# RWKV stage of a two-block transformer kernel: chunk states of pair p beside the inverse of p+1 and the preparation of p+2

## The chip, the cores and the metric

One core of one Trainium2 chip. The metric is the device time of one execution in microseconds (us); lower is better.

## What is computed

Two transformer blocks over 512 tokens of width 1024, in fp32. The change touches one branch of the first block, the RWKV-7 time mix over 16 heads of 64 channels. Its inputs come from a projection and are shifted by a token; then a state of 64x64 per head runs over the tokens:

```python
f = f + (f_prev - f) * mu                       # token shift, per channel
a = sigmoid(a0 + fa @ w_a2); g = sigmoid(fg) @ w_g2
kk = k * k_k; kk = kk / max(norm(kk), 1e-12)    # per head
k = k * (1 + (a - 1) * k_a)
def step(state, (r, w, k, v, kk, a)):           # per head, 512 tokens
    sa = state @ (-kk)
    state = state * w + outer(sa, kk * a) + outer(v, k)
    y = state @ r
y = ((y - mean) * rsqrt(var + 64e-5)) * ln_w + ln_b   # per head
y = (y + sum(r * k * r_k) * v) * g
```

The rest (two attentions, gates, output projections, two feed-forward layers) stays as it is.

## The kernel before

Every engine has its own written-out program; they meet at semaphores, and each engine takes its instructions in program order. Weights come in 126 units of 128x2048 through a ring of 3 places: a DMA, then `hi(n)` on ScalarE rounds a unit to fp32r (L975), GpSimd subtracts to get the low part (L479), and TensorE does three products for each (`mm3`, L488 to L490).

The heads are taken in 8 pairs, a pair over the 128 partitions, its 512 tokens in 4 chunks of 128. The work of a pair:
- *Projection.* `side_unit` gives two weight units (r and k, then v and a gate). One piece is three 512-column products; a unit is 16 pieces. Both go to PSUM banks 0 and 1. ScalarE copies them out (`take_rk`, `take_vg`), and VectorE shifts them by a token (`shift`, L1591, L1592).
- *Preparation* (`prep`): small projections for decay, rate and gate, sums over heads by a product with `ones_head`, ScalarE sigmoids, roots and exponentials, VectorE products. The root of the key norm is a square root and a reciprocal of a 128x512 tile (L1616); the norm of the output has the same (L1691).
- *Tokens and grams*: transposes (L818), then products of 256 columns (L832, L833), taken out of PSUM by `copy_predicated` (L1712).
- *Inverse*: a triangular matrix for each chunk and head is inverted in 7 levels. A level is 8 small products (`level_x`, L732), an addition on VectorE (L1651), 16 products (`level_t`, L742, L744) and four copies on ScalarE (L1200, L1201); VectorE makes the mask product for the next level (`level<-gram,consts`, L1654). Two refining products follow (`refine_u`, `refine_c`).
- *Chunks* (`chunks`): for each of the 4 chunks in turn a right-hand side (L778, L779), its copy on ScalarE, the solution (L785), its copy on VectorE, and the state's update (L791, L792, L1676, L1677). The output of the chunk is L782, L795, L796.
- *Norm* of the output, and gate: L805, L810, L1685 to L1701.

`pair_step` of pair p runs: levels 2 to 6 and refining of p beside the preparation of p+1, the chunks of p, then tokens, grams and levels 0 and 1 of p+1 beside the norm of p. Pieces of the projection of p+2 are put in by `fill(2)` and `fill(1)`. Pairs 6 and 7 have no projection left to put in. Behind the last pair `rwkv_hi` and `rwkv_lo` split all 8 pairs at once, beside the products `attb`; then `rwkvb` follows.

Of the kernel before, what the change touches and what calls it, by code (L numbers as in the profile page):

```python
# [9 lines left out]
F32R = mybir.dt.float32r  # L10
I32 = mybir.dt.int32
# [4 lines left out]
P = 128  # L16
# [10 lines left out]
L2_EPS2 = 1e-24  # L27
# [70 lines left out]
CCOLS = [("ident", P), ("eps", 1), ("ln_eps", 1), ("ones_head", P), ("ones", P), ("strict_incl", 2 * P),  # L98
# [7 lines left out]
N_CCOLS = _c  # L106
TOE_LEN = 640


def constants():  # L110
# [12 lines left out]
    put("strict_incl", np.concatenate([(p <= c), (p < c)], 1).astype(np.float32))  # L123
# [41 lines left out]
def build(nc, x, wpack, lora_wa, lora_g, params, rel_bias, post_gains, sink, ctab, btab, icount, out):  # L165
# [7 lines left out]
    with ExitStack() as ctx:  # L173
# [23 lines left out]
        def sem(name):  # L197
# [14 lines left out]
        C = fixed("consts", [P, N_CCOLS])  # L212
        PR = fixed("params_sb", [P, N_PCOLS])
        stat = fixed("stat", [P, 64])
        OAT = fixed("att_out", [P, 2, T])
        SG = place("gate_act", [P, 2, T], at=top[0] - 4 * 2 * T)[0]
        OAl = place("att_lo", [P, 2, T], F32R, at=top[0] - 4 * 2 * T)[0]
# [13 lines left out]
        G0 = place("gate0_tile", [P, 2, T], at=r.at)[0]  # L231
        LRAW = r("lora_raw", [P, 2, T + 1])
# [7 lines left out]
        ORW = place("rwkv_out", [P, PAIRS, T], at=x_at)[0]  # L240
        r = Region(y_at)
        RAW = r("rkv", [P, 2, 3, T + 1])
# [5 lines left out]
        LM = r("mid_decay", [P, 2, 2, NT])  # L248
        assert r.at <= y_at + 4 * NT * D
# [11 lines left out]
        X2 = r("work_x", [P, T])  # L261
        KB = r("kb", [P, 2, T])
# [3 lines left out]
        GM = [r(f"gram{h}", [P, NT, 4, P]) for h in range(2)]  # L266
# [7 lines left out]
        ORh = place("rwkv_hi", [P, KT, T], F32R, at=base + K16)[0]  # L274
        ORl = place("rwkv_lo", [P, KT, T], F32R, at=base + 2 * K16)[0]
# [53 lines left out]
                             "pt_taken", "pv_full", "o_taken"))  # L329
        sink_in, ic_in, x_back, gain_in, out_done = (  # L330
# [9 lines left out]
        side_taken = sem("side_taken")  # L340
        gate_tile = sem("gate_tile_ready")
        gate_stored = sem("gate_stored")
        pad_ready = sem("pad_ready")
        gate_back = [sem("gate0_back"), sem("gate1_back")]
        gate0_tile, gate0_stored = sem("gate0_tile_ready"), sem("gate0_stored")
        ident_r = sem("ident_r_ready")
        pair_open = sem("pair_open")
        rs = {n: sem(n) for n in ("z_full", "sig_ready", "zg_full", "g_ready", "sq_ready", "ss_full", "nrm_ready", "sqrt_ready",
                                  "rk_ready", "bonus_full", "csm_ready", "exps_ready", "rakb_ready",
# [23 lines left out]
        def side(pair, u):  # L373

            return 1 + 2 * pair + u + (UNITS["gate0"] if pair >= 2 else 0)
# [107 lines left out]
        def _(pe):  # L483
# [175 lines left out]
            def side_unit(j):  # L659
# [3 lines left out]
                if j:  # L663
                    pe.wait_ge(side_taken, j)
# [1281 lines left out]
```

## Time and profile before

| | |
|---|---|
| median of 3 runs | 2293.16 us (2291.77 to 2301.49) |
| profiled execution | 2285.9 us, its span 2284.1 us, mean granted clock 0.922 |
| TensorE busy | 2047.9 us, 90% of the span |
| VectorE busy | 929.9 us, 41% |
| ScalarE busy | 759.3 us, 33% |
| GpSimd busy | 579.3 us, 25% |
| RWKV stage | from 301.5 us, first product of the preparation, to 1005.5 us, first product of `attb` |

A matmul's end is modelled, so TensorE's busy share hides short waits. Start-to-start distances of consecutive instructions tell more. An fp32 product shows as two instructions, an fp32r product as one. The granted clock is a share of 2.4 GHz; a low stretch is at half of that.

### The profile page before, as it was taken

The numbers are of one execution on the slowest core, as the hardware profiler recorded it, in microseconds if no ns is written. First come the engines' busy times: TensorE is split into PE (matmuls) and PEld (weight loads), VectorE is DVE, ScalarE is ACT, GpSimd is POOL, SyncE is SP. The second block draws the span as 40 slices with busy tenths as digits, with TensorE's granted clock in tenths as the row PEclk, the third lists the DMA queues.
The fourth block names the chain that finished last, engine by engine and source line by source line (L and its number), as shares of the span: only waits on it lengthen the run. The fifth ranks groups of instructions, "written<-read, shape, count | busy, mean of one in ns | idle before, by whom it ended". The sixth has DMA issues, their size and how long they took to land.

```text
span 2284.1 us, 23519 instructions
## 1 busy us (share of the span) xinstructions
PE 2047.9 (90%) x9988; PEld 1629.4 (71%) x9988; DVE 929.9 (41%) x1400; ACT 759.3 (33%) x1097; POOL 579.3 (25%) x130
## 2 busy tenths in 40 slices
PE   6999969889888988878799989979898888999897
PEld 5877757667666767756688868867666667888786
DVE  2033366865866864632301134440554322111243
ACT  4234533433433422211422222242455223212222
POOL 2422210010110100003244434424121423444342
PEclk9999989999999975569899999989999999999999
DMA  4611210010100120012222222222111212222221
GB/s 158 211 56 60 79 60 22 26 44 19 44 26 19 44 97 1 0 39 100 79 79 97 106 74 92 93 74 97 38 56 42 106 52 87 105 98 92 76 98 67
DMA packets 31067, 160.66 MB, mean 70 GB/s; under 512 B 3023, under 2 KB 5327, under 8 KB 14708
## 3 DMA queue, kind: packets, MB, share of 16 engines
q1 hardware_dynamic: 19244, 135.53, 16.9%
q10 hardware_dynamic: 11720, 23.63, 3.0%
q8 instruction: 79, 1.29, 0.2%
q14 instruction: 24, 0.20, 0.0%
HBM read 152.57 MB, written 10.25 MB: 71 GB/s over the span
## 4 chain that ended last, share of the span: by engine, by line
PE 76%; DVE 13%; ACT 5%; issue 5%; POOL 1%; POOLq 0%; DMA 0%; DVEq 0%; ACTq 0%
PE ps L488 20%; PE ps L489 19%; PE ps L490 19%; PE ps L573 2%; PE ps L551 2%; PE ps L742 2%; PE ps L732 2%; PE ps L744 2%; ACT w_hi L975 2%; DVE work_t L1698 1%; PE ps L778 1%; PE ps L779 1%; PE ps L785 1%; DVE gram L1712 1%; POOL w_lo L479 1%
## 5 line engine op out<-in xcount | busy, mean ns | idle before, releaser
L479 POOL TENSOR_TENSOR w_lo<-w_raw,w_hi 128x2048 fp32r<-128x2048 f32 x126 | 579.1, 4597 | 1673.7 <-ACT w_hi L975 1673.6
L488 PE MATMUL ps<-ht_hi,w_hi 128*128 128x512 f32 x1240 | 518.6, 418 | 21.8 <-DVE ht_lo L1453 14.0
L490 PE MATMUL ps<-ht_hi,w_lo 128*128 128x512 f32 x1240 | 492.7, 397 | 0.0
L489 PE MATMUL ps<-ht_lo,w_hi 128*128 128x512 f32 x1240 | 492.3, 397 | 0.0
L975 ACT ACTIVATE w_hi<-w_raw 128x2048 fp32r<-128x2048 f32 x126 | 241.2, 1915 | 550.4 <-PE ps L490 519.9
L488 PEld LDWEIGHTS ps<-ht_hi,w_hi 128*128 128x128 f32 x1240 | 238.8, 193 | 98.4 <-issue 40.5
L490 PEld LDWEIGHTS ps<-ht_hi,w_lo 128*128 128x128 f32 x1240 | 238.0, 192 | 52.0
L489 PEld LDWEIGHTS ps<-ht_lo,w_hi 128*128 128x128 f32 x1240 | 239.3, 193 | 46.2 <-issue 4.2
L488 PE MATMUL ps<-w_hi,hid_hi 128*128 128x512 f32 x432 | 173.9, 402 | 24.1 <-DVE hid_lo L1796 16.5
L1796 DVE TENSOR_TENSOR hid_lo<-hidden,hid_hi 128x1024 fp32r<-128x1024 f32 x27 | 114.8, 4264 | 151.8 <-ACT hid_hi L1302 151.8
L489 PE MATMUL ps<-w_lo,hid_hi 128*128 128x512 f32 x432 | 172.8, 400 | 0.0
L490 PE MATMUL ps<-w_hi,hid_lo 128*128 128x512 f32 x432 | 172.8, 400 | 0.0
L488 PEld LDWEIGHTS ps<-w_hi,hid_hi 128*128 128x128 f32 x432 | 83.1, 192 | 45.2 <-issue 17.2
L488 PE MATMUL ps<-w_hi,ht_hi 128*128 128x512 f32 (+2 forms) x256 | 89.5, 350 | 25.4 <-DVE ht_lo L1761 17.6
L1200 ACT ACTIVATE tinv_t<-ps 128x512 fp32r<-128x512 f32 x96 | 57.7, 601 | 137.7 <-PE ps L744 135.0
L489 PEld LDWEIGHTS ps<-w_lo,hid_hi 128*128 128x128 f32 x432 | 83.3, 193 | 19.3
L490 PEld LDWEIGHTS ps<-w_hi,hid_lo 128*128 128x128 f32 x432 | 82.8, 192 | 19.5
L489 PE MATMUL ps<-w_lo,ht_hi 128*128 128x512 f32 (+2 forms) x256 | 88.9, 347 | 0.0
L490 PE MATMUL ps<-w_hi,ht_lo 128*128 128x512 f32 (+2 forms) x256 | 88.7, 346 | 0.0
L1791 DVE TENSOR_TENSOR hidden<-ps,gate_act 128x1024 f32<-128x1024 f32 x16 | 19.6, 1224 | 159.8 <-ACT gate_act L1344 159.8
L732 PEld LDWEIGHTS ps<-tinv,level 128*128 128x128 f32 x384 | 60.6, 227 | 32.0 <-issue 22.2
L732 PE MATMUL ps<-tinv,level 128*128 128x128 f32 x384 | 69.1, 326 | 12.9 <-ACT tinv L1201 6.9
(246 smaller groups left out, 2868.4 us busy)
## 6 DMA issues: line engine op xcount, KB each, us to landing
w_raw<-in_wpack SPq DMA_DIRECT2D x126, 1024.0 KB, 4.8
bias_skewed_dram<-bias_rows_dram ACTq DMA_DIRECT2D x1, 3840.0 KB, 24.2
toe<-bias_skewed_dram ACTq DMA_DIRECT2D x1, 3072.0 KB, 13.8
x_res<-in_x SPq DMA_DIRECT2D x4, 512.0 KB, 5.0
gate_dram<-gate_tile ACTq DMA_DIRECT2D x8, 256.0 KB, 4.5
gate_dram<-gate_tile ACTq DMA_DIRECT2D x4, 512.0 KB, 5.1
merged<-gate_dram ACTq DMA_DIRECT2D x1, 2048.0 KB, 11.4
gate<-gate_dram ACTq DMA_DIRECT2D x1, 2048.0 KB, 12.5
```

What stands on the lines that cost most here:

```text
L479: nc.gpsimd.tensor_tensor(Wl[:, slot, :], raw[:, slot, :], f32(Wh[:, slot, :]), ALU.subtract).then_inc(lo_ready, 1)
L488: mm(dst, wh, ah, start=first, stop=False)
L489: mm(dst, wh, al, start=False, stop=False)
L490: return mm(dst, wl, ah, start=False, stop=last)
L551: last = mm(bank(s["bank"], s["n"]), s["q"], s["k"], start=True, stop=True)
L573: last = mm(out_slot(a, i), v, PT[:, j, :], start=j == 0, stop=j == len(it["vals"]) - 1)
L732: last = mm(ps[:, 4 + h, t * P:(t + 1) * P], Mb[h][:, t, :], Tb[h][:, t, :] if lv else identR[:], start=True, stop=True)
L742: mm(ps[:, 6 + h, t * P:(t + 1) * P], Xb[h][:, t, :], TT[h][:, t, :], start=True, stop=True)
L744: last = mm(ps[:, 4 + h, t * P:(t + 1) * P], TT[h][:, t, :], Xb[h][:, t, :], start=True, stop=True)
L975: actf(Wh[:, n % RING, :], raw[:, n % RING, :], ACT.Copy).then_inc(hi_ready, 1)
L1200: actf(TT[h][:].rearrange("p a b -> p (a b)"), bank(6 + h), ACT.Copy)
L1796: v.tensor_tensor(HIl[:, 2 * g:2 * g + 2, :], HID[:, 2 * g:2 * g + 2, :], f32(HIh[:, g % RING, :, :]), ALU.subtract).then_inc(hid_lo, 1)
```

## The change

All loops of the stage become one `step(p)` for p from -2 to 7 on every engine. In a step the chunks of pair a = p, the whole inverse with tokens and grams of pair b = p+1, and the preparation of pair c = p+2 are put into one another by hand.
- The projection goes by halves of a unit (8 pieces, one output tile), all into bank 0 in the later pairs. Each half waits until the half before it was taken out. `early` are the last two halves of c (v and gate), `late` the first two of c+1 (r and k).
- Token shift at evacuation: ScalarE copies a half, scaled by mu, into one tile (`stage`), and VectorE adds the unscaled part from PSUM, shifted by a token (`shift`, one instruction and a column).
- Head sums for roots become products with the data as weights and 2 columns of `ones_head`, so that a root is 128x8; ScalarE widens it (`widen`) and 4 transposes bring it back (`spread`). Both 128x512 reciprocals go.
- The grams that the inverse needs are made on their own at the start of a step (`inverse_grams`); the other products of 128 columns follow later (`grams`). `refine_u` loses its identity product, and the add after `refine_c` takes twice the old value instead.
- The right-hand sides of both heads share bank 3, with a wait `head_done` between.
- `rwkv_hi` and `rwkv_lo` of pairs 0 to 6 are made before the last step. The reload of `x_res` is issued later, and `absdist` is loaded on its own in the second block.

The core of the diff, indentation as in the file, first TensorE's functions, then ScalarE's, then VectorE's:

```diff
+            def side_half(n, b, behind):
+                u = UNIT0["lora"] + n // 2
+                if n % 2 == 0:
+                    pe.wait_ge(lo_ready, u + 1)
+                if behind >= 0:
+                    pe.wait_ge(*half_taken(behind))
+                for k in range(KT):
+                    wh, wl = rows_of(u, KT, k, n % 2 * P, P)
+                    last = mm3(bank(b), wh, wl, HTh[:, k, :], HTl[:, k, :], k == 0, k == KT - 1)
+                    if k == KT - 1:
+                        last.then_inc(side_full, 1)
+                    yield
...
+            def head_sums(dst, src):
+                for t in range(NT):
+                    last = mm(dst[:, 2 * t:2 * t + 2], src[:, tok(t)], root_cols(ones_head), start=True, stop=True)
+                return last
...
+            def spread(dst):
+                for t in range(NT):
+                    last = nc.tensor.transpose(dst[:, tok(t)], NX[:, tok(t)], ident)
+                return last
...
+            def inverse_grams(b):
+                w("kb1_ready", 1, b, 1)
+                for t in range(NT):
+                    for h in range(2):
+                        last = mm(ps[:, 4 + h, tok(t)], KB[heads(h), 1, tok(t)], RA[b % 2][heads(h), t, 1, :],
+                                  start=True, stop=True)
+                inc(last, "agram_full")
...
+            def step(p):
+                a, b, c = p, p + 1, p + 2
+                has_a, has_b, has_c = 0 <= a, 0 <= b < PAIRS, c < PAIRS
+                if p == -2:
+                    early = later_halves(GATE0 + 6, GATE0 + 8)
+                else:
+                    early = later_halves(half(c, 2), half(c, 2) + (2 if 2 <= c < PAIRS else 0))
+                late = later_halves(half(c + 1, 0), half(c + 1, 0) + (2 if 2 <= c + 1 < PAIRS else 0))
+                if has_b:
+                    inverse_grams(b)
+                if has_c:
+                    lora_z(c, 0)
+                if has_a:
+                    chunk_rhs(a, 0)
+                advance(early, 2)
+                if has_a:
+                    chunk_solve(a, 0)
+                if has_b:
+                    level_x(b, 0)
+                advance(early, 2)
+                if has_a:
+                    chunk_out(a, 0)
+                for t in range(1, NT):
+                    if has_b:
+                        level_x(b, t)
+                    if has_a:
+                        chunk_rhs(a, t)
+                    advance(early, 1)
+                    if has_c:
+                        if t == 1:
+                            lora_z(c, 1)
+                        elif t == 2:
+                            key_sums(c)
+                        else:
+                            key_roots(c)
+                    if has_a:
+                        chunk_solve(a, t)
+                    if has_b:
+                        level_t(b, t)
+                    advance(early, 1)
+                    if has_a:
+                        chunk_out(a, t)
+                    advance(early, 2)
+                if has_b:
+                    level_x(b, 4)
+                    to_tokens(b, 0)
+                    to_tokens(b, 1)
+                advance(late, 1)
+                if has_a:
+                    mean(a)
+                if has_b:
+                    level_t(b, 4)
+                advance(late, 3)
+                if has_b:
+                    level_x(b, 5)
+                    to_tokens(b, 2)
+                advance(late, 1)
+                if has_a:
+                    variance(a)
+                if has_b:
+                    level_t(b, 5)
+                    grams(b, 0)
+                advance(late, 3)
+                if has_b:
+                    level_x(b, 6)
+                    grams(b, 1)
+                advance(late, 1)
+                if has_a:
+                    norm_roots(a)
+                if has_b:
+                    level_t(b, 6)
+                    grams(b, 2)
+                advance(late, 2)
+                if has_c:
+                    gate_z(a, c)
+                advance(late, 1)
+                if has_b:
+                    refine_u(b)
+                    grams(b, 3)
+                advance(late, 2)
+                if has_c:
+                    bonus(c)
+                if has_b:
+                    refine_c(b)
+                advance(late, 2)
+                assert next(early, None) is None and next(late, None) is None
...
+            def stage(n, b, buf, mu):
+                act.wait_ge(side_full, n + 1)
+                actf(buf, bank(b), ACT.Copy, scale=pcol("mu", mu)).then_inc(staged, 1)
...
+            def take_gate1(pair, b):
+                n = half(pair, 3)
+                act.wait_ge(side_full, n + 1)
...
+            def widen(root):
+                return actf(NX[:].rearrange("p (t h c) -> p t h c", h=2, c=HD),
+                            root[:].unsqueeze(3).to_broadcast([P, NT, 2, HD]), ACT.Copy)
...
+            def shift_part(pair, part):
+                if part == 0:
+                    act.wait_ge(gate_stored, 16 * pair)
+                else:
+                    act.wait_ge(*half_taken(half(pair, part) - 1))
+                stage(half(pair, part), 0, GT[:], 8 * part + pair)
...
+            def step(p):
...
+                if c + 1 < PAIRS:
+                    lora_weights(c + 1)
+                if early:
+                    shift_part(c, 1)
+                    hi(UNIT0["lora"] + half(c, 0) // 2 + 2)
...
+                if has_b:
+                    level(b, 1)
+                if early:
+                    shift_part(c, 2)
+                elif p == -2:
...
+                if has_c:
+                    key_root(c)
+                if has_a:
+                    rhs(a, 3)
+                if has_c:
+                    widen_keys(c)
+                if has_b:
+                    level(b, 3)
...
+                if early:
+                    take_gate1(c, 0)
+                    hi(UNIT0["lora"] + half(c, 2) // 2 + 2)
+                elif p == -2:
+                    act.wait_ge(gate0_stored[0], 16 * 4)
+                    take_gate0(7, 0, GT[:])
+                    act.wait_ge(gate0_stored[1], 16 * 4)
+                    hi(UNIT0["lora"] + (GATE0 + 6) // 2 + 2)
+                if has_b:
+                    tokens(b, 0)
+                    tokens(b, 1)
+                    level(b, 4)
+                if has_c:
+                    exponentials(c)
+                if has_b:
+                    tokens(b, 2)
+                    level(b, 5)
+                if late:
+                    shift_part(c + 1, 0)
+                if has_a:
+                    deviation(a)
+                    widen_norm(a)
+                if has_b:
+                    level(b, 6)
+                if has_c:
+                    if a >= 0:
+                        act.wait_ge(pair_open, a + 2)
+                    gate_copy(c)
+                    inverse_exponential(c)
...
+            def shift(n, dst, b, buf, mu):
+                dve.wait_ge(staged, n)
+                v.scalar_tensor_tensor(dst[:, 1:T], ps[:, b, 1:T], OM[:, mu:mu + 1], buf[:, 0:T - 1], ALU.mult, ALU.add)
+                v.tensor_scalar(dst[:, 0:1], ps[:, b, 0:1], OM[:, mu:mu + 1], None, ALU.mult).then_inc(shifted, 1)
+                dve.wait_ge(shifted, n)
...
+            def level_mask(b, lv):
...
+            def inverse_grams(b):
+                w("agram_full", 1, b, 1)
+                v.memset(stat[:, 40:41], 0.0)
+                for h in range(2):
+                    ins = v.copy_predicated(GA[h][:], mask[:, P:2 * P].unsqueeze(1).to_broadcast([P, NT, P]), b3(4 + h))
+                order(ins)
+                level_mask(b, 0)
...
+            def step(p):
...
+                if has_b:
+                    inverse_grams(b)
+                if early:
+                    shift_part(c, 1)
+                if has_a:
+                    solved(a, 0)
+                if has_b:
+                    level_first(b)
+                if has_a:
+                    state(a, 0)
...
+                if has_b:
+                    level_x(b, 2)
+                if early:
+                    shift_part(c, 2)
...
+                if has_b:
+                    level_x(b, 4)
+                if has_a:
+                    centred(a)
+                if has_b:
+                    level_mask(b, 5)
+                    level_x(b, 5)
+                if has_c:
+                    queries(c)
+                if has_b:
+                    level_mask(b, 6)
+                    grams(b, 0)
+                if has_a:
+                    norm_root(a)
+                if late:
+                    shift_part(c + 1, 0)
+                if has_b:
+                    level_x(b, 6)
+                    grams(b, 1)
+                if has_a:
+                    normed(a)
+                if has_b:
+                    grams(b, 2)
+                    refine_e(b)
+                    grams(b, 3)
+                if has_c:
+                    bonus(c)
+                if has_b:
+                    refine_t(b)
+                    state_zero(b)
+                if has_c:
+                    keys(c)
```

## Rows read from the trace of the kernel before

**Rows 1.** Stretches: time, PE, PEld, DVE, ACT, POOL busy, clock, DMA share, GB/s

```profile
301.50:380.10 78.60, 66.15 (x344) 53.47 (x344) 62.00 (x93) 30.93 (x48) 4.54 (x1) 0.85 0.07 25
380.10:462.10 82.00, 71.70 (x458) 55.78 (x458) 60.05 (x91) 31.40 (x51) 9.14 (x2) 0.98 0.10 32
...
708.10:791.20 83.10, 73.98 (x469) 57.63 (x469) 60.13 (x91) 32.23 (x53) 10.08 (x3) 0.96 0.11 38
791.20:886.20 95.00, 81.22 (x406) 63.38 (x406) 60.15 (x91) 28.66 (x47) 8.12 (x2) 0.72 0.17 60
886.20:969.10 82.90, 72.25 (x346) 61.61 (x345) 41.70 (x72) 22.49 (x40) 0.00 (x0) 0.55 0.00 1
969.10:1005.50 36.40, 25.75 (x124) 17.40 (x124) 9.95 (x17) 2.39 (x6) 0.00 (x0) 0.52 0.00 0
1005.50:1020.50 15.00, 14.11 (x48) 11.02 (x49) 8.00 (x5) 3.62 (x1) 0.00 (x0) 0.80 0.01 1
```

**Rows 2.** Timeline of TensorE: start, us, engine, line, operation

```profile
532.56 0.40 PE L488 MATMUL ps<-ht_hi,w_hi 128*128 128x512 f32 x1
...
533.25 0.56 PE L742 MATMUL ps<-tinv_t,xinv 128*128 128x128 f32 x4
...
534.99 0.44 PE L488 MATMUL ps<-ht_hi,w_hi 128*128 128x512 f32 x1
...
555.40 0.43 PE L778 MATMUL ps<-state,ra 64*128 64x64 f32 x2
...
557.30 0.66 PE L785 MATMUL ps<-rhs_sb,tinv_full 128*128 128x64 f32 x4
557.76 0.48 PE L488 MATMUL ps<-ht_hi,w_hi 128*128 128x512 f32 x1
...
558.63 0.34 PE L791 MATMUL ps<-sa_sb,b_chunk 128*64 128x64 f32 x4
...
559.50 0.50 PE L488 MATMUL ps<-ht_hi,w_hi 128*128 128x512 f32 x1
...
600.00 0.69 PE L710 MATMUL ps<-lora_in,lora_w 64*128 64x512 f32 x1
...
601.07 1.11 PE L732 MATMUL ps<-tinv,level 128*128 128x128 f32 x8
602.01 0.44 PE L488 MATMUL ps<-ht_hi,w_hi 128*128 128x512 f32 x1
```

**Rows 3.** Groups between 544.1 and 626.1: count, busy us, mean ns, idle before

```profile
L1201 ACT ACTIVATE tinv<-ps 128x512 fp32r<-128x512 f32 x12 | 7.3, 606 | 0.0
...
L1654 DVE TENSOR_TENSOR level<-gram,consts 128x512 fp32r<-128x512 f32 x10 | 6.4, 682 | 0.0
L1712 DVE COPY_PREDICATED gram<-consts,ps 128x512 f32<-128x512 int32 x8 | 5.1, 713 | 6.6 <-issue 6.6
...
L975 ACT ACTIVATE w_hi<-w_raw 128x2048 fp32r<-128x2048 f32 x2 | 3.8, 1911 | 0.0
...
L1691 DVE RECIPROCAL work_x<-work_x 128x512 f32<-128x512 f32 x1 | 3.3, 3343 | 0.0
...
L1190 ACT ACT_TABLE_LOAD x1 | 1.3, 1283 | 0.0
```

**Rows 4.** Timeline of GpSimd and VectorE where they meet

```profile
337.87 4.54 POOL L479 TENSOR_TENSOR w_lo<-w_raw,w_hi 128x2048 fp32r<-128x2048 f32 x1 [36.93 <-ACT w_hi L975]
...
338.65 0.69 DVE L1651 TENSOR_TENSOR xinv<-ps,consts 128x512 fp32r<-128x512 f32 x1 [0.15 <-PE ps L732]
339.26 3.70 DVE L1654 TENSOR_TENSOR level<-gram,consts 128x512 fp32r<-128x512 f32 x1
...
591.46 5.11 DVE L1698 TENSOR_TENSOR work_t<-work_t,bonus 128x512 f32<-128x512 f32 x1
```

**Rows 5.** Timeline of TensorE behind the last pair

```profile
992.98 2.07 PE L805 MATMUL ps<-work_e,consts 128*128 128x512 f32 x2 [0.71 <-ACT work_e L1216]
...
1005.56 0.80 PE L488 MATMUL ps<-att_hi,w_hi 128*128 128x512 f32 x1 [6.92 <-DVE rwkv_out L1701]
```

More of the change, by code:

```diff
@@ L248, in build @@
         LM = r("mid_decay", [P, 2, 2, NT])
+        NR = [r(f"root{i}", [P, NT, 2]) for i in range(2)]
         assert r.at <= y_at + 4 * NT * D
@@ L1264, in _ @@
[L1264 to L1265 removed]
+            lora_weights(0)
+            for p in range(-2, PAIRS - 2):
+                step(p)
             act.dma_start(MG[:], gate0_dram.rearrange("k p t -> p k t")).then_inc(gate_back[0], 16)
@@ L1656, in refine, with parts, shift_part, key_squares @@
-            def refine(q, off, ahead, o):
-                w = pairwise(q, off)
+            def parts(c):
+                return (RKV[:, c % 2, j, :] for j in range(3))
+            def shift_part(c, part):
+                shift(2 + 3 * c + part + 1, RKV[:, c % 2, part, :], 0, GT, 8 * part + c)
+            def key_squares(c):
+                rr, kk_, vv = parts(c)
+                order(v.tensor_scalar(KK[:], kk_, pcol("k_k", c), None, ALU.mult))
+                inc(v.tensor_tensor(X2[:], KK[:], KK[:], ALU.mult), "sq_ready")
@@ new lines, in decay_sums, with key_scale @@
+            def decay_sums(c):
+                w("sig_ready", 2, c, 1)
+                for t in range(NT):
+                    ins = v.tensor_tensor_scan(CS[:, t * P:(t + 1) * P], ones, SZ[:, t * P:(t + 1) * P], 0.0,
+                                               ALU.mult, ALU.add)
+                order(ins)
+            def key_scale(c):
+                rr, kk_, vv = parts(c)
+                w("sig_ready", 2, c, 2)
+                order(v.tensor_scalar(T1[:], Ab[:], -1.0, pcol("k_a", c), ALU.add, ALU.mult))
+                order(v.scalar_tensor_tensor(kk_, T1[:], 1.0, kk_, ALU.add, ALU.mult))
@@ L1741, in _ @@
-            for step in range(8):
-                prep(0, 0, step, order)
-            grams(0, 0)
-            for lv in range(3):
-                level(0, 0, lv)
-            for q in range(PAIRS // 2 - 1):
-                pair_step(q, 0, True, order)
-                pair_step(q, 1, True, order)
-            pair_step(PAIRS // 2 - 1, 0, True, order)
+                    ins = v.copy_predicated(GM[h][:, t, :, :].rearrange("p a b -> p (a b)"), mask, ps[:, 2 + h, 0:3 * P])
+                inc(ins, "gram_taken")
```

901 lines of the change are left out of this document (418 added, 483 removed).

## The prediction

> **What bounds the kernel now.** I read first the busy shares of the page: TensorE 90%, the others under half. So the question is how well TensorE's program is filled in the RWKV stage. For that I cut the stage at the first product of each pair's chunks (L778) and asked for busy times by stretch [rows 1]. The reader should see four parts. The start, to the first chunks, takes 78.6 us. Then come five periods from 380.1 to 791.2, of 82.0 us four times and 83.1 once, with TensorE idle for some 10 us of each (82.0 - 71.7) and the clock near full. Then two periods of 95.0 and 82.9 us at a clock of 0.72 and 0.55, though they hold little or no projection. Last come 36.4 and 15.0 us behind the chunks of pair 7.
>
> The second view is TensorE's timeline, read as distances between starts [rows 2]. A piece of projection takes 0.69 us (532.56 to 533.25), `level_t` 1.74 (to 534.99), `level_x` 0.94 (601.07 to 602.01). The right-hand sides with the state's part of the output take 1.90 (555.40 to 557.30), the solution 0.46 (to 557.76), the rest of a chunk 0.87 (558.63 to 559.50). An fp32 product of 512 columns takes 1.07, and the two half-height ones L710 and L711 take these 1.07 together (600.00 to 601.07). In a steady period of 82.0 us idle time is near 10; some ten short waits lose about 0.2 each that the modelled ends hide; a clock of 0.96 costs 2 to 3. Real work is then about 67 us: 32 pieces are 22.1, seven `level_x` and six `level_t` 17.0, four chunks 12.9, and the rest is preparation, grams, transposes and refining. More overlap has at most 15 us of 82 to win in a steady period, and more only where the clock is low.
>
> **The work of TensorE, part by part.** The two small projections are now apart: +1.1. Two sums of 512 columns become 4 fp32 products of 2 columns each. No row shows one; from above I bound it by the 512-column form (1.07), from below by nothing, and take the nearest row, L785 with 8 instructions in 2 x 0.46: 0.9 a sum, so -0.3 for both. The Trainium skill (TensorE: Matmul & The Clock Gate, section "Wait — 56ns, not 53.3ns?") gives small products a floor of 25 ns, or 62 ns of sequencer time. By that a sum would be about 0.5 us, an estimate, and the stage some 6 us shorter than by the row; no run here shows it yet. Eight transposes for two roots: +0.9 (a `level_x` of 8 such products is 0.94). The identity products of `refine_u`: -1.1. Grams have a quarter fewer columns but 24 products in place of 16: between -0.4 and +1.9. With more changes of shape I take +0.7 us in all, so 67.7 a step.
>
> **VectorE and ScalarE.** VectorE loses 2 reciprocals of 3.34 and three shift subtractions; what is left is about 74 operations, most of 0.69 [rows 3], some 51 us a step. ScalarE gets two more table loads of 1.28 and two widening copies: about 38 us a step [rows 3]. Neither is the bound by its sum. What counts is where TensorE's order waits for theirs.
>
> **The waits in a steady step.** I went through the three orders, with TensorE's first `inverse_grams` product at 0.
> - 0.9 us before 0: it waits for `keys(c)` of the last step, which comes behind `bonus`, `refine_t`, a table load and two exponentials.
> - At 3.7 TensorE comes to `early`, the half for v. Bank 0 must be free: `stage` of the half for k is early on ScalarE, but its `shift` on VectorE stands behind `inverse_grams`, two `copy_predicated` (to 2.7) and two mask products. Without GpSimd that would be over at 4.9. But ScalarE's `hi` of 1.91 follows `stage` directly, so GpSimd subtracts from about 2.5 to 7.0. Rows 4 show what that does: while GpSimd works from 337.87, `xinv<-ps,consts` (one SBUF input) runs at 338.65 in 0.69, and the mask product `level<-gram,consts` (two SBUF inputs) at 339.26 takes 3.70 and ends only when GpSimd does; L1698 takes 5.11 beside the next one [rows 4]. So both masks end at 8.4, `shift` at 9.2, and TensorE stands for 5.5 us. Queued behind this wait are `chunk_solve`, `level_x(b, 0)` and with them everything of VectorE.
> - 0.8 at `level_x(b, 1)`, which waits for four operations and a mask after the late start.
> - 1.2 at the half for the gate: its `shift` stands behind `decay_sums`, `key_scale` and `level_x(b, 2)`.
> - 0.5 at the first `late` half, for a sigmoid with its table load.
> - 2.2 at `level_x(b, 5)`: the second `hi` puts GpSimd at about 49 to 53.4, and the square in `centred` (two SBUF inputs) waits, the mask behind it too.
> - 2.0 at the second `late` half: its `shift` stands behind `norm_root`, which waits for ScalarE's root and table load.
> - some 0.5 in small ones.
> Together 13.6 us, against about 12.5 in a period of before (10 idle, 2.5 hidden). The overlap takes away the waits of tokens, grams and first levels, and the single bank and the held port bring as many back. 67.7 + 13.6 + about 1 for the clock is 82.3: five steps give +1 us. Bounds: a step of 76 if the port costs nothing, and 87 if each of ten hand-offs is 0.5 later.
>
> **The start.** Before: 78.6 us. Step -2 now holds two gate halves whose tile goes to DRAM before ScalarE goes on to `hi` and the exponentials: about 29 us. Step -1 has the whole inverse of pair 0 with projection only from level 4 on, so its first four levels run at the pace of their chain, about 5 us each: 57. With 2 to the chunks 88.6: +10, bounds 0 and +18.
>
> **Pairs without projection.** Step 5 has its first half like a steady step (44.6); the second without `late` is chain, VectorE and the second held port: 34. Step 6 has chunks and inverse alone. At full clock I count 62, at half clock 84; between them by the clock of these stretches (0.55 and 0.72) [rows 1]: 74. Together 153 against 95.0 + 82.9: -25, bounds -45 and -8.
>
> **The end.** Between the last mean and `attb` lie 12.6 us (992.98 to 1005.56) [rows 5], 3.3 of them a reciprocal, and the output products no longer wait in the queue for the gated result: about -3. Splitting one pair instead of 8 lets `attb` run without VectorE's 4 us: -2. Together -5, bounds -9 and 0.
>
> Sum: +1 + 10 - 25 - 5 = -19. The profiled execution took 2285.9, so 2267 on its scale; the median of the runs is 7.3 above it, so 2274 on that of the runs.
>
> **The rivals.**
> *The held port falls beside the masks, not on them.* If `hi` ends before the masks start or after them, the 5.5 becomes 1.2 and the 2.2 goes: 6.5 x 5 steps and 2 in step 5 = -35, so 2239. For it: operations that read PSUM pass freely, as at 338.65 [rows 4], and many of a step's do. Against: `hi` stands right behind `stage`, and the masks right behind the grams. The Trainium skill (SBUF — State Buffer, section "SBUF: two separate sides") makes it a lock on the shared pair held for a whole instruction, against operations of VectorE with two SBUF inputs or in a two-port mode; by that rule the row holds for every mask, and this rival needs luck in time; the trace agrees (339.26, 3.70 us).
> *The clock* (the other side). TensorE stands for 5.5 us in one piece in each step. The stretch 791.2 to 886.2 ran at 0.72 and took 95.0 us [rows 1]. If steady steps are granted 0.88 and not 0.97, work of 67.7 costs 67.7 x (1/0.88 - 1/0.97) = 7.1 more, x 5 = +36: 2310. It decides from 6 us a step on. For it: the new wait is longer than any in a steady period now. Against: dense pieces follow it, and small chunk products no longer come in one block.
> *Nothing at all.* Steady steps as forecast, but low clock eats the overlap in steps 5 and 6 (-8) and the start costs its 10 or more: about 2292.
>
> **Chances.** Forecast, 2258 to 2288: 0.42. Port rival: 0.24. Clock rival: 0.22. Nothing: 0.12. A change under 0.5% (11.5 us) is about what a measurement cannot tell from none. Three quarters of the forecast and all of the first rival are faster: 0.56; a quarter of the forecast and 0.09 of the last are the same: 0.19; the rest 0.25 slower. The range for 8 in 10 is 2228 to 2312, from the port rival's and the clock rival's numbers; the forecast's own is 2258 to 2288.
>
> **What would show it.** Right: chunk starts of pairs 0 to 5 some 82 us apart; one wait of 4 us or more on `shift` at the first `early` product of each step, with a mask of over 3 us beside GpSimd; the last two periods 79 and 74; the start near 89. Wrong: masks of 0.7 us only, steps of 76 or less, or a granted clock under 0.9 in steady steps. What would upset the sum most is a wrong place of GpSimd's pieces, for it is paid five times.

## The result and the profile after

The kernel after took 2312.57 us in the median of 10 runs (2308.44 to 2316.82), beside 2297.0 for the kernel before in 10 runs taken with it. The ratio is 1.0065, with a 95% interval of 1.0035 to 1.0096: slower, and 39 us above the forecast of 2274. The profiled execution took 2311.98 us, 26.1 more than the one of before (2285.9). By the medians the change costs 15.6 us: the profiled execution of before was among its faster ones, so the account below, which is made from the two profiles, shows some 10 us more than a typical pair would. One execution in all the experiments, the 2312.56 us among the four of e2, at a granted clock of 0.897, counts as a slow one and is left out of e2's ratio.

The page of the kernel after, parts 1 and 2 (the slices are 58 us long):

```profile
PE 2081.4 (90%) x10212; PEld 1683.2 (73%) x10212; DVE 875.5 (38%) x1427; ACT 792.1 (34%) x1140; POOL 578.9 (25%) x130
...
PEclk8999977888879797559889999989999988999999
```

VectorE fell as meant, from 929.9 to 875.5. TensorE, with fewer full-width products, shows 33.5 us more: either more work or the same work on a slower clock. The clock row points to the second; the kernel before had there

```profile
PEclk9999989999999975569899999989999999999999
```

Cut at the first product of each pair's chunks, as in [rows 1] (columns as there), the start, two of the five steady steps and the two steps without projection are:

```profile
303.20:403.40 100.20, 81.93 (x391) 64.53 (x392) 50.13 (x96) 37.34 (x57) 4.50 (x1) 0.73 0.07 22
492.00:582.10 90.10, 80.17 (x489) 65.80 (x487) 53.91 (x96) 35.35 (x56) 9.09 (x2) 0.85 0.09 28
582.10:676.50 94.40, 84.61 (x488) 69.43 (x487) 53.84 (x95) 35.28 (x56) 9.09 (x2) 0.82 0.09 27
855.10:938.90 83.80, 71.53 (x438) 60.16 (x437) 52.86 (x90) 32.47 (x53) 9.46 (x2) 0.79 0.10 33
938.90:1009.50 70.60, 68.21 (x357) 59.92 (x356) 34.24 (x68) 22.61 (x37) 0.00 (x0) 0.57 0.14 51
```

Over the whole program, in us, with the same instruction as mark in both kernels (so the periods of before differ by 0.1 to 2 us from [rows 1], whose cuts at 544.1 to 886.2 lie up to 2 us beside the first chunk products):

| part | before | after | difference | forecast |
|---|---|---|---|---|
| up to the start of the stage | 301.5 | 303.2 | +1.7 | 0 |
| start, to the first chunks | 78.6 | 100.2 | +21.6 | +10 |
| five steady steps | 409.1 | 451.6 | +42.5 | +1 |
| two pairs without projection | 180.0 | 154.4 | -25.6 | -25 |
| end of the stage | 51.4 | 46.2 | -5.2 | -5 |
| behind the branch | 1263.5 | 1254.6 | -8.9 | 0 |
| sum | | | +26.1 | -19 |

Two terms came out within a microsecond. The start, the steady steps and, with no change there, the part behind the branch did not. TensorE's waits in the step from 492 (engine, line, releaser: total, times, longest) do not explain it:

```profile
PE ps L511 <- DVE rkv L1683: 7.5, 3, 5.3
PE ps L817 <- DVE level L1792: 2.1, 1, 2.1
PE ps L805 <- DVE kb L1787: 0.3, 1, 0.3
```

That is 9.9 us, with the 5.3 and the 2.1 where the forecast had put 5.5 and 2.2, and the cause of the longest is in VectorE's timeline (start, us):

```profile
491.92 0.71 DVE L1798 COPY_PREDICATED gram_inv<-consts,ps 128x512 f32<-128x512 int32 x1
...
492.66 5.40 DVE L1792 TENSOR_TENSOR level<-gram_inv,consts 128x512 fp32r<-128x512 f32 x2
497.98 0.74 DVE L1682 SCALAR_TENSOR_TENSOR rkv<-ps,one_less_mu,gate_tile 128x511 f32<-128x511 f32 x1
```

The first two masks take 5.40 together while GpSimd holds the port (it works 4.50 from 492.41), and `shift` comes behind them. What lies behind the wait is the reading that matters, TensorE's timeline:

```profile
499.00 0.77 PE L511 MATMUL ps<-ht_hi,w_hi 128*128 128x512 f32 x1 [5.29 <-DVE rkv L1683]
499.56 0.63 PE L512 MATMUL ps<-ht_lo,w_hi 128*128 128x512 f32 x1
499.99 0.63 PE L513 MATMUL ps<-ht_hi,w_lo 128*128 128x512 f32 x1
500.41 0.63 PE L511 MATMUL ps<-ht_hi,w_hi 128*128 128x512 f32 x1
```

The starts are 0.43 us apart, where three such products took 0.69 in [rows 2]. The granted clock around the stand, in windows (columns as above):

```profile
492.00:494.40 2.40, 1.71 (x13) 1.20 (x11) 2.37 (x3) 1.33 (x3) 1.99 (x1) 1.00 0.77 324
494.40:499.00 4.60, 0.00 (x1) 0.03 (x1) 4.45 (x4) 1.25 (x2) 2.51 (x1) 0.51 0.00 0
499.00:508.10 9.10, 9.10 (x39) 7.51 (x40) 4.34 (x9) 0.00 (x0) 0.00 (x0) 0.50 0.00 0
508.10:512.00 3.90, 3.90 (x28) 2.88 (x24) 2.40 (x5) 0.28 (x1) 0.00 (x0) 1.00 0.02 4
```

TensorE stands from 493.7 to 499.0. The clock falls to 1.2 GHz within the stand, at 494.4, and stays there until 508.1, over 9 us of work. What this costs has to be counted with care. Half clock costs time only while TensorE works: a us of work at half clock is half a us lost, and the 4.6 us of half clock in the stand cost nothing beyond the wait. Multiplying the length of a step by what its mean clock lacks, 90.1 x (1 - 0.85) = 13.5, counts them twice. The traces, with the stretches at half clock laid over TensorE's busy time, give for the five steady steps together, in us:

| | before | after | difference |
|---|---|---|---|
| TensorE idle | 47.8 | 49.5 | +1.7 |
| lost to the clock while it worked | 13.5 | 57.6 | +44.1 |
| work, at full clock | 347.8 | 344.5 | -3.3 |
| sum | 409.1 | 451.6 | +42.5 |

Counted so, work is 68 to 70 us in every steady step of before, of after and of all the variants below, whatever its clock (73 in e3, which adds work), so the account holds together. The steps are longer by the clock. The overlap saved no idle time in them (9.9 us a step, 9.6 before), as the forecast had it, and work is 0.7 us a step less. In the start, 9.7 us were lost to the clock before and 20.7 after: 11 of its +21.6. Of the rest 5.8 are idle time and 4.7 work.

### The profile page after: what moved, and what is told of

It reads as the page before. It is cut to its first block, busy times and chain, and to the rows that moved or that the text cites. A ratio compares the mean times of both kernels' runs of the same rounds, so it can differ in the third digit from the quotient of the medians.

```text
span 2310.2 us, 24099 instructions
## 1 busy us (share of the span) xinstructions
PE 2081.4 (90%) x10212; PEld 1683.2 (73%) x10212; DVE 875.5 (38%) x1427; ACT 792.1 (34%) x1140; POOL 578.9 (25%) x130
## 4 chain that ended last, share of the span: by engine, by line
PE 80%; DVE 10%; ACT 6%; issue 2%; POOL 1%; DMA 0%; POOLq 0%; ACTq 0%; DVEq 0%
PE ps L511 21%; PE ps L512 19%; PE ps L513 19%; PE ps L817 2%; PE ps L825 2%; PE ps L827 2%; DVE level L1792 2%; PE ps L596 2%; PE ps L574 2%; ACT w_hi L1079 2%; DVE norm_sq L1851 1%; POOL w_lo L502 1%; PE ps L867 1%; PE ps L748 1%; PE ps L588 1%
## 5 line engine op out<-in xcount | busy, mean ns | idle before, releaser
L511 PE MATMUL ps<-ht_hi,w_hi 128*128 128x512 f32 x1240 | 524.7, 423 | 58.0 <-DVE rkv L1683 43.3
L512 PE MATMUL ps<-ht_lo,w_hi 128*128 128x512 f32 x1240 | 499.8, 403 | 0.0
L513 PE MATMUL ps<-ht_hi,w_lo 128*128 128x512 f32 x1240 | 499.6, 403 | 0.0
L512 PEld LDWEIGHTS ps<-ht_lo,w_hi 128*128 128x128 f32 x1240 | 243.2, 196 | 44.1 <-issue 1.4
L1792 DVE TENSOR_TENSOR level<-gram_inv,consts 128x512 fp32r<-128x512 f32 x112 | 101.0, 942 | 0.6
L817 PE MATMUL ps<-tinv,level 128*128 128x128 f32 x384 | 63.3, 313 | 19.3 <-DVE level L1792 17.7
```

Of the source, the lines that this page charges most:

```text
L511: mm(dst, wh, ah, start=first, stop=False)
L512: mm(dst, wh, al, start=False, stop=False)
L513: return mm(dst, wl, ah, start=False, stop=last)
L817: last = mm(ps[:, 4 + h, tok(t)], Mb[h][:, t, :], Tb[h][:, t, :] if lv else identR[:], start=True, stop=True)
L1792: inc(v.tensor_tensor(Mb[h][:], GA[h][:], lmask(lv), ALU.mult), "m_ready")
```

## Experiments

Theory A: a stand of TensorE of a few us is what lowers the clock behind it, and the held port is what makes the longest one. Theory B: the new order itself lowers the clock, because small products of chunks, levels and sums now lie between the pieces everywhere. Each kernel below is the kernel after with an edit. "Steps" are the five steady ones of the profiled execution.

**e1_port.** ScalarE rounds the first weight unit of a step at the end of the step before, so GpSimd's subtraction no longer lies on the first masks.

```diff
                 if early:
                     shift_part(c, 1)
-                    hi(UNIT0["lora"] + half(c, 0) // 2 + 2)
...
                     level(b, 6)
+                if late:
+                    hi(UNIT0["lora"] + half(c + 1, 0) // 2 + 2)
```

> The first weight rounding of a step on ScalarE (and with it GpSimd's subtraction) moves from the start of the step to the end of the step before, where VectorE works from PSUM. Three theories for the eight us by which a steady step of the changed kernel (90) is longer than forecast (82). A, the wait: TensorE stands 5.3 us for the token shift because GpSimd holds up the masks, and this stand is also what lowers the clock behind it. Then the wait falls to about 1.2, the low stretch behind it goes, the clock of a steady step rises from 0.85 to 0.90 or more, and a step takes 81 to 83: 2270 to 2278 in all. B, small products: the clock falls because the chunks' small products are now spread over half of the step, whatever the waits. Then only the wait goes, about 4 us a step, the clock stays at 0.85: 86 a step, about 2290. C, sheer work: TensorE's program is longer than counted; then a step gains 4 as in B, and busy time stays.

**e2_shift_first.** The port stays held, but VectorE makes the `shift` of the second half (k), for which the first `early` product waits, ahead of the grams and masks.

```diff
+                if early:
+                    shift_part(c, 1)
                 if has_b:
                     inverse_grams(b)
-                if early:
-                    shift_part(c, 1)
```

> VectorE takes the token shift of the second half ahead of inverse_grams; GpSimd stays where it is. The wait at the first product of early goes wholly, but the masks are still held to about 7 us, so a wait of about 2 us shows at level_x(b,0). A: a stand of 5.3 becomes one of 2, gain 3.3 a step plus part of the clock, 84 to 86 a step, 2278 to 2290. B: 3.3 a step without any change of clock, 87 a step, about 2295.

**e3_filler.** The cause of the wait stays; TensorE gets 16 spare products of 512 columns (results unused) to do in it.

```diff
                 if has_a:
                     chunk_rhs(a, 0)
+                if has_a and 2 <= c < PAIRS:
+                    for i in range(16):
+                        mm(bank(6 + i % 2), identR[:], HTh[:, i % KT, :], start=True, stop=True)
                 advance(early, 2)
```

> Adds work and takes nothing away: 16 products of 512 columns in fp32r (about 3.7 us at full clock) into PSUM banks that nobody reads, put where TensorE stands 5.3 us in each step with projection. They fit into the wait, so waits and work behind stay as they were and only the clock can change. A: the stand no longer lowers the clock; each of six steps gets 3 to 4 us shorter in spite of more work: about 2290 to 2295. B: no shorter step, clock behind the wait as low as before: 2312 within 4, or longer.

**e4_both.** e1 and e2 together, and on VectorE the `shift` of the first late half, for which the second waits, ahead of `norm_root`.

> Both moves together, and the shift of the first late half ahead of the root of the norm on VectorE (a wait of 2.0 us). A: three waits of 5.3, 2.0 and (unchanged) 2.3 become one of 2.3; a step takes 78 to 80, the clock is over 0.90: about 2255. B: 7 us a step less and the clock as now, 83 a step: about 2275.

What they gave (median of the runs; ratio to the kernel before with its interval; before took 2298.91 beside them):

| kernel | us | ratio | steps, us | their clocks |
|---|---|---|---|---|
| e1_port | 2274.48 | 0.991 [0.987, 0.995] | 82.5 85.3 85.3 85.3 91.6 | .92 .88 .88 .88 .81 |
| e2_shift_first | 2267.94 | 0.985 [0.976, 0.995] | 92.1 82.8 81.9 82.0 81.9 | .81 .92 .94 .94 .94 |
| e3_filler | 2304.61 | 1.002 [0.999, 1.006] | 89.6 85.1 90.8 86.7 90.8 | .89 .94 .87 .92 .87 |
| e4_both | 2256.93 | 0.984 [0.977, 0.990] | 83.5 84.7 85.0 83.7 84.6 | .88 .86 .86 .88 .86 |

e2 moves two instructions on one engine, removes a wait of 5.3 us, and four of its steps are 82 to 83 us: 7 to 13 shorter than those of the kernel after. Its windows, the first step and the third:

```profile
404.20:496.30 92.10, 85.72 (x487) 70.21 (x486) 53.92 (x95) 35.38 (x56) 9.12 (x2) 0.81 0.09 28
579.10:661.00 81.90, 75.05 (x487) 61.10 (x486) 53.62 (x95) 35.26 (x56) 9.13 (x2) 0.94 0.10 31
```

The same 487 products are 85.72 us busy in one and 75.05 in the other, and the waits are the same (6.4 and 6.8 us, none above 2.1): TensorE's busy time is a measure of its clock here. Both theories had expected less of e2 (2278 to 2290 and 2295 us). e1 came in the range of A (2270 to 2278), but with 0.88 in three steps and 0.81 in the last, where A had expected 0.90 or more. e3 adds 3.5 us of work to a step (16 x 0.22), and its median is still 8 us under that of the kernel after, though the two intervals overlap; A had expected 2290 to 2295 and B 2312, and it came between. The kernel after is at half clock from 2 to 5 us behind each step's first chunk product to 12 or 16; in e1 and e3 no step has a stretch that begins there, in e2 the first two have a short one. In e3 three begin at 15 and two at 27 or later. This supports A: the low stretch at that wait belongs to the wait. It also shows that another can come in its place: e1 has one from 12 to 22 in four steps.

e4 speaks for B beside it. It has the fewest waits of all,

```profile
PE ps L817 <- DVE level L1793: 2.4, 2, 2.1
PE ps L754 <- ACT norm_sq L1271: 0.6, 1, 0.6
PE ps L511 <- DVE rkv L1684: 0.5, 1, 0.5
PE ps L805 <- DVE kb L1788: 0.3, 1, 0.3
```

3.8 us in a step of 85.0, and its steps are not shorter than e2's, at a clock of 0.86:

```profile
570.50:655.50 85.00, 81.16 (x488) 66.31 (x487) 49.78 (x95) 35.37 (x55) 9.15 (x2) 0.86 0.09 30
```

It has two stretches at half clock in each step. One, some 10 to 14 us long from about 52, begins behind the wait of 2.1. The other, of 7 to 14 us, begins 10 to 22 us into a step, in a place with no wait above 0.6. Against e2 it is 11 us lower in the median, but the intervals of the ratios overlap, and the profiled executions (2266.28 and 2268.44) hardly differ; three of e4's four runs were at 2257. In time that is what A expected (2255), in steps and clock nearer to B (83 us, clock unchanged).

**e5_port2** (e4, and the second `hi` moved behind `widen_norm(a)`, so that GpSimd leaves `norm_sq` alone).

> e4_both, and the second weight rounding of a step moved behind the widened root of the norm too, so that GpSimd no longer runs beside the square of the centred output and the mask behind it. In e4_both the wait of 2.1 us at level_x(b,5) is the last large one and the clock falls behind it in each step (low from about 50 to 65 us after the chunks' start), mean 0.86. A, waits lower the clock: the low stretch near 50 to 65 goes with the wait, clock 0.92, a step 84.5 to about 79: 2228 to 2235. B, small products lower it: only the 2.1 us go, 82.5 a step, about 2247.

2263.18 us, 0.987 [0.984, 0.991], beside 2286.31 for before; no gain on e4, where A expected 2228 to 2235 and B 2247. (e5 to e8 and, beside a before of 2296.37, e9 and e10 ran on another chip than e1 to e4: compare ratios rather than times.) Steps of 82.4 to 84.6 at 0.90 to 0.92. The wait of 2.1 fell to 0.3, but both subtractions of GpSimd now follow each other, 9.22 us from 629.51, VectorE's last operations on the output are held beside them, and grams stood behind these. TensorE's timeline at that place:

```profile
641.14 1.23 PE L905 MATMUL ps<-ra,kb 64*128 64x256 f32 x4 [5.29 <-DVE gram L1846]
642.16 0.64 PE L907 MATMUL ps<-ra,kb 64*128 64x128 f32 x4
...
644.17 0.63 PE L511 MATMUL ps<-ht_hi,w_hi 128*128 128x512 f32 x1
...
648.10 0.39 PE L513 MATMUL ps<-ht_hi,w_lo 128*128 128x512 f32 x1
```

and VectorE's, just ahead of it:

```profile
629.72 4.65 DVE L1864 TENSOR_SCALAR rwkv_out<-rwkv_out,params_sb 128x512 f32<-128x512 f32 x1
634.40 4.87 DVE L1865 TENSOR_TENSOR rwkv_out<-rwkv_out,bonus 128x512 f32<-128x512 f32 x1
```

The low stretch went with the wait: from 50 to 65 us of a step to 70 to 80. This is the clearest sign for A: another place, another instruction, the same 5.3 us, and the clock falls 3 to 5 us after the stand begins. But the price differs: here the stretch is 6.8 us long and the steps are as short as those of e4, which has no such stand, while in the kernel after it was 6.8 to 13.7. So a stand of 5.3 us has no fixed price. The port is a cost that one moves, and not only onto operations with two SBUF inputs: L1864 is a `tensor_scalar` with one, which takes 0.55 in e4 and took 4.65 here.

**e6_roots** (e4 with both roots as before: sums over 512 columns, root and reciprocal of 128x512, no `widen`, no `spread`).

> e4_both with one part of the change undone: both head sums are products of 512 columns with ones_head again, root and reciprocal are on 128x512 tiles (3.3 us twice on VectorE), no widening and no transposes. B, small products lower the clock: key sums (8 instructions of 2 columns) and variance sums stand just where the low stretches of e4_both lie, so those shrink and the step gets shorter or stays in spite of 6.7 us more on VectorE: 2250 or less. A: nothing in the clock changes but by new waits; VectorE's reciprocals come late for level_x(b,3) and for the last products, two waits of 1 to 3 us a step: 2265 to 2280. A price for the part itself: by the rows a sum of small products and a transposed root cost TensorE 0.9 + 0.45 against 1.07.

2283.34 us, 0.999 [0.996, 1.002]: 20 us slower than e5, and by the ratios 1.5% slower than e4. In the profiled execution the start is 3.8 longer, the two pairs behind 6.8, the end 2.3 and what follows the branch 6.2; the steps are 84.0, 89.3, 81.8, 85.0 and 85.9. `xinv` waits behind a reciprocal; TensorE's waits from 661:

```profile
PE ps L823 <- DVE xinv L1808: 5.3, 2, 4.3
PE ps L815 <- DVE level L1786: 2.1, 2, 1.8
```

So the change's small roots are worth their place (A had expected 2265 to 2280 us, B 2250 or less), by this profile mostly outside the steady steps. The 6.2 behind the branch are not theirs: nothing was changed there, and 129.5 us of it were at half clock, beside 109.1 in e4.

In clock, though, e6 speaks for B. In its five steps TensorE is idle for 41.2 us, beside 18.7 in e4, and yet it loses less to the clock: 40.6 us beside 56.3, at 0.92, 0.85, 0.94, 0.90 and 0.88. Every steady step of e4, e5, e7, e8 and e9 has a stretch at half clock that begins 10 to 23 us into it; in e6 one of five has. The chunk products there are the same, and so is a wait of 0.5 us at 20.5; what differs on TensorE are the sums of 2 columns and the transposes. They can't be the whole cause. In 11 of those 25 steps the stretch begins ahead of the first sum, in eight of them by 15 to 18 us; in this step of e4 it is 0.4 us, the clock falls at 592.1:

```profile
592.10 0.61 PE L513 MATMUL ps<-ht_hi,w_lo 128*128 128x512 f32 x1
592.51 1.70 PE L748 MATMUL ps<-consts,work_x 128*128 128x2 f32 x8
```

**e7_place** (e4, with `hidden`, `hid_lo` and `hid_hi` 896 bytes higher, where the kernel before has them). It asks about the -8.9 us behind the branch, where no instruction was changed.

```diff
-        r = Region(base)
+        r = Region(base + 896)
...
-        HIl = place("hid_lo", [P, 2 * FF1_GROUPS, T], F32R, at=base)[0]
+        HIl = place("hid_lo", [P, 2 * FF1_GROUPS, T], F32R, at=base + 896)[0]
```

> e4_both with the tiles hidden, hid_lo and hid_hi placed 896 bytes higher, as far up as the kernel before had them (its table of constants was larger by so much). Nothing else. Behind the RWKV stage the changed kernel is 9 us shorter than the kernel before though no instruction there was changed; 6.8 of them lie in the two down projections, whose 1296 products take 395 ns and not 400. If the place of the operands does that, the down phases get 6 to 7 us longer again, to 185.3 and 129.3 us: about 2263. If it is the clock or chance, they stay at 181 and 126.5: 2257.

2274.98 us, 0.992 [0.988, 0.996], where 2263 was expected if the place did it. The profiled execution, 2287.33, is the slowest of ten from 2262.86. Behind the branch it has 1267.0 us in place of e4's 1253.6. Not all of these 13.4 us are the operands' place: 129.0 us of that part were at half clock, beside 109.1 in e4. The down products of the feed-forward layers between 1400 and 2200 us (busy, mean ns), of the kernel before, of after and of e7:

```profile
L489 PE MATMUL ps<-w_lo,hid_hi 128*128 128x512 f32 x233 | 93.1, 400 | 0.0
```

```profile
L512 PE MATMUL ps<-w_lo,hid_hi 128*128 128x512 f32 x239 | 94.4, 395 | 0.0
```

```profile
L512 PE MATMUL ps<-w_lo,hid_hi 128*128 128x512 f32 x224 | 90.2, 403 | 0.0
```

These means mix both clocks. The distance from start to start at full clock is free of that: 232 ns before, 227 in the kernel after and in e4, 232 in e7. The down projections of the two feed-forwards take, from first to last start, 185.8 and 129.8 us before, 181.7 and 127.0 after, 181.6 and 127.0 in e4, 187.5 and 130.0 in e7 (of whose 187.5 some 3.5 us more than in e4 are at half clock). So 6.9 of the -8.9 are a gift of where tiles came to lie, and no part of the schedule. Why an address matters to these products was not tried.

**e8_start** (e4; in step -1 the first 8 late pieces go between levels 0 to 3, where TensorE has nothing else).

> e4_both, with the first late half of step -1 (8 pieces, 5.5 us of work) put into the levels 0 to 3 of the first pair's inverse, which have nothing beside them. The start, 100 us from the first product to the first chunks against 78.6 before, has a clock of 0.73. By A, work in the gaps of the chain keeps the clock up as well: 8 to 12 us less, start about 90, 2246. By the sum of work alone it saves 5.5 at most: 2252. If the start is bound by its chain on VectorE and ScalarE whatever TensorE does: no change, 2257.

2263.29 us, 0.988 [0.983, 0.992], against e4 no gain in the runs (the intervals overlap), where 2246, 2252 or 2257 was expected. In the profiled execution the start falls from 100.0 to 96.8, at a clock of 0.77 in place of 0.73. The first levels are a chain through VectorE and ScalarE; pieces between them fill it and do not shorten it much.

**e9_cover** (e4) and **e10_cover2** (e2): `to_tokens(b, 2)` and one piece go ahead of `level_x(b, 5)`, into the stand of 2.1 us.

```diff
                 advance(late, 3)
                 if has_b:
+                    to_tokens(b, 2)
+                advance(late, 1)
+                if has_b:
                     level_x(b, 5)
-                    to_tokens(b, 2)
-                advance(late, 1)
```

> e4_both with two pieces of other work moved ahead of level_x(b, 5), into the one stand of 2.1 us that is left in its steps: the four transposes of to_tokens(b, 2) and one piece of projection, 1.1 us at full clock in all. e4_both has steps of 83.5 to 85.0 us at a clock of 0.86 to 0.88, waits of only 3.8 us, and a low stretch at 50 to 65 us of each step, right behind this stand; another lies at 10 to 32 with no stand ahead of it. Theory A (a stand lowers the clock): the stand falls to 1.0 us or less, the stretch at 50 to 65 is gone or halved, the clock of the steps is 0.90 or more, steps of 80 to 82, 2240 to 2250 us in all. Theory B (stretches of small products lower it, whether TensorE stands or not): the stretch stays where it is, clock 0.86 to 0.88, steps no more than 1 us shorter, 2252 to 2262.

> e2_shift_first with the same two pieces moved ahead of level_x(b, 5). e2_shift_first has steps of 82 us at 0.94 in its last four, with low stretches of 7 and 3.4 us, the second right behind the stand of 2.1 us at level_x(b, 5), and a first step of 92 at 0.81. Theory A: the second stretch goes, steps of 80 to 81 at 0.96, 2255 to 2262 us. Theory B: steps as they are, 2264 to 2272.

e9: 2248.8 us, 0.980 [0.975, 0.985], the lowest median here; e4's interval overlaps it. The profiled execution, 2257.34 at 0.911, was the slowest of the four (the others 2247 to 2250 at 0.915 and 0.916). Steps of 82.5, 79.4, 82.3, 82.0, 81.9 at 0.87 to 0.91. The longest wait is 1.0:

```profile
PE ps L817 <- DVE level L1794: 1.3, 2, 1.0
PE ps L754 <- ACT norm_sq L1272: 0.6, 1, 0.6
PE ps L805 <- DVE kb L1789: 0.3, 1, 0.3
```

2.2 us of waits in a step of 81.9, and the clock is still 0.87 (of the five, 0.87 to 0.91):

```profile
648.20:730.10 81.90, 79.63 (x487) 63.72 (x486) 49.53 (x95) 35.25 (x55) 9.16 (x2) 0.87 0.10 32
```

The stretch at half clock behind `level_x(b, 5)` shrank from 10 to 14 us to 3 to 7 in four steps; the one that lies between 10 and 32 stayed, 10 to 14 us long, in one step with a second of 7 behind it. e10: 2267.23 us, 0.987 [0.983, 0.992], the same as e2; its steps are 87.9, 81.7, 81.8, 85.0 and 80.2. Here A expected 2255 to 2262 and B 2264 to 2272, so B had it. In e9 the time and the steps came by A and the clock by B. Neither theory is enough alone.

## Why the prediction was wrong

**The step that failed** is "67.7 + 13.6 + about 1 for the clock is 82.3". A steady step of after (the one of 90.1 us) is 9.9 of waits that the profile shows, 11.3 lost to the clock while TensorE worked, and 68.8 of work, in which hidden waits are included. Work was right within about 1 us and the waits within 4; the clock was 11.3 and not 1, and it is paid five times over. The term was also set without a reason: the same text puts the clock at 2 to 3 us in a period of before, and then at less in a kernel with a longer stand. The rival for it was the case that came: it had 0.88 and +7.1 a step, and the steps ran at 0.82 to 0.87 and took +8.5 a step over before (8.8 for the clock, 0.3 more idle, 0.7 less work). That its 2310 us in all lies so near to 2312.57 is in part luck: the start was 12 us worse and the part behind the branch 9 us better than the sum had them, and the median of after lies 0.6 us, and not 7.3, above its profiled execution. The rival was put aside with "dense pieces follow it, and small chunk products no longer come in one block". The first reason fails at 499.00, where six dense products in a row run at half clock behind the stand. The second fails in e4 and e9: mixed among the pieces, the small products go with a clock of 0.86 to 0.91 when little waits.

**The start** was +21.6 and not +10. Step -2 took 34.4 (29 forecast), step -1 63.9 (57), and 1.9 (2) came to the chunks. The clock is 0.73, and no term of the start stood for it; 11 of the 21.6 are clock, as worked out above.

**The waits**, the longest ones, were as forecast: the 5.3 on `shift` at the first `early` product (5.5), the two masks at 5.40 beside GpSimd, 2.1 at `level_x(b, 5)` (2.2), where `norm_sq` takes 4.56, and 1.7 at the second `late` half (2.0). The small ones came to less, 9.9 in all in place of 13.6. The rival of the port that falls beside the masks is refuted for the kernel after; e1 made it true, and its first four steps are 3 to 9 us shorter than those of after, at 0.88 to 0.92 and not at 0.97.

**The small sums.** A sum is four products of 2 columns, eight instructions, and takes 0.81 us from start to start at full clock (forecast 0.9) and 1.56 at half clock: 0.10 and 0.20 an instruction. By the floor that the Trainium skill gives for small products (TensorE: Matmul & The Clock Gate, section "Wait — 56ns, not 53.3ns?") a sum would be 0.2 to 0.5 us, an estimate, eight times 25 or 62 ns. The trace shows more than either.

**Pairs without projection and the end** came out at -25.6 (-25) and -5.2 (-5). The first is partly luck, two errors that cancel: step 5 took 83.8 and step 6 70.6, with 79 and 74 forecast. **Behind the branch** no term stood, and -8.9 came; 6.9 of it are the down projections, which e7 takes away again.

**What stays open.** A stand of 5.3 us lowers the clock: taken away in three ways (e1, e2, e3), and moved in e5, the low stretch went with it each time. But low stretches also come where no wait is above 0.6, 10 to 22 us into the steps of e4 and e9, behind chunk products of 64 columns that follow one another at 0.36 us, head by head. Whether these small products do it was only argued; no run changed them alone. e6, which changed the sums of 2 columns, no longer had most of these stretches, but it changed waits too. The Trainium skill (TensorE: Matmul & The Clock Gate, section "A second HAM failure mode: psum-queue depth-cycling") tells of a kernel whose clock swings because the engine idles for moments between groups of products; that could be so in e4 and e9, and no run here separates it from B. Nor is it known why e2 has one step of 92.1 before four of 82, with the same products and nearly the same waits, and only the clock apart.

## What to carry to other kernels

Count a wait of several us on TensorE for its own length and for the clock behind it: here taking the wait of 5.3 us away made steps 7 to 13 us shorter, by moving two instructions on VectorE (e2), though in another place the same stand cost less (e5). Count half clock only where the engine works, or what lies in the wait is counted twice. Waits that are taken away can come back as half clock (e4 waits less than e2, and four of its five steps ran at a lower clock), so read the granted clock of each stretch beside its idle time, and price an order by both. When GpSimd and VectorE share a port, moving GpSimd's piece moves the wait; look at what it lands on before you count the gain.

## What the hardware showed beyond the forecast

- Half clock can last longer than the stand in which it begins: 5.3 us idle, then 9 us more until 508.1, in which each 512-column product takes 0.43 us in place of 0.23.
- At a clock of 0.87, a step with 2.2 us of visible waits loses 81.9 x 0.13 = 10.6 us to the clock, five times what it waits.
- 896 bytes in the place of an operand are worth 5 ns on a product of 512 columns (227 and 232 from start to start at full clock), about 7 us over the 1296 products of the two down projections.
- Eight fp32 instructions of 2 columns with 128x128 weights cost 0.81 us, and eight fp32r instructions of 128 columns 0.94 ([rows 2]): fewer columns gain next to nothing here.
- GpSimd's subtraction also holds a `tensor_scalar` of VectorE with one SBUF input: 4.65 us in e5, 0.55 in e4.
